# One 512-column product over high and low tokens in the FFN up projections, gated product in PSUM, last up tile one place forward

## What is computed

```
def conv_gated_mlp(hn, w_up, conv_w, conv_b, w_down):
    u = causal_dwconv(hn @ w_up, conv_w, conv_b)
    gate, val = jnp.split(u, 2, axis=-1)
    return (jax.nn.silu(gate) * val) @ w_down
...
        f = (jax.nn.silu(h @ w_ffn_gate[l]) * (h @ w_ffn_up[l])) @ w_ffn_down[l]
```

## Time and profile before

| | us |
|---|---|
| median of 3 runs | 1210.48 (1210.32 to 1210.68) |
| the profiled execution | 1210.57, span 1208.6 |
| PE busy | 1183.3, 98% of the span |
| POOL busy | 881.0, 73% |
| DVE busy | 703.3, 58% |
| ACT busy | 701.7, 58% |

### The profile page before, as it was taken

The page is one execution under the profiler, slowest core; times in us unless marked ns, Lnnn a source line. Parts: engine busy times, 40 slices in busy tenths (PEclk is TensorE's granted clock), DMA queues, the critical chain, the costliest instruction groups (busy, mean ns, idle before and its releaser), DMA issues.

```text
span 1208.6 us, 23310 instructions
## 1 busy us (share of the span) xinstructions
PE 1183.3 (98%) x8146; PEld 1069.2 (88%) x8146; DVE 703.3 (58%) x1520; ACT 701.7 (58%) x1315; POOL 881.0 (73%) x371
## 2 busy tenths in 40 slices
PE   8999999999999999999999999999999999999996
PEld 7998898779999998889999998888798888999995
DVE  5668677456666666546666666293363525444454
ACT  7777677465555557656555656665366445444442
POOL 5847643287988987537889889888786475988882
PEclk9999999999999999999999999999999999999998
DMA  8688522256766656415566665666566344665650
GB/s 284 191 165 201 158 89 89 70 159 207 228 192 190 201 183 187 139 46 164 176 207 190 186 198 158 192 208 193 158 186 196 102 145 119 210 190 177 190 155 36
DMA packets 61354, 202.90 MB, mean 168 GB/s; under 512 B 6480, under 2 KB 13008, under 8 KB 61152
## 3 DMA queue, kind: packets, MB, share of 16 engines
q1 hardware_dynamic: 53712, 193.51, 52.3%
q10 hardware_dynamic: 7568, 8.39, 3.6%
HBM read 197.68 MB, written 4.19 MB: 167 GB/s over the span
## 4 chain that ended last, share of the span: by engine, by line
PE 70%; issue 12%; POOL 10%; DVE 5%; ACT 2%; DMA 0%; POOLq 0%; SPq 0%; DVEq 0%; ACTq 0%
PE bank L183 17%; PE bank L184 16%; PE bank L185 16%; POOL wlo L167 9%; PE solve L185 5%; PE solve L184 5%; PE solve L183 5%; DVE flo L587 1%; ACT whi L163 1%; ACT xhi L306 1%; PE bank L1771 0%; PE bank L1772 0%; DVE resid L2195 0%; PE bank L1468 0%; DVE scr L2190 0%
## 5 line engine op out<-in xcount | busy, mean ns | idle before, releaser
L167 POOL TENSOR_TENSOR wlo<-raw,whi 128x1024 fp32r<-128x1024 f32 x362 | 874.6, 2442 | 294.3 <-ACT whi L163 293.2
L163 ACT ACTIVATE whi<-raw 128x1024 fp32r<-128x1024 f32 x362 | 379.6, 1055 | 134.5 <-PE bank L185 120.0
L183 PE MATMUL bank<-xhi,whi 128*128 128x256 f32 (+1 forms) x936 | 269.8, 288 | 1.2 <-DVE xlo L312 1.0
L184 PE MATMUL bank<-xlo,whi 128*128 128x256 f32 (+1 forms) x936 | 264.6, 283 | 0.0
L185 PE MATMUL bank<-xhi,wlo 128*128 128x256 f32 (+1 forms) x936 | 264.5, 283 | 0.0
L183 PEld LDWEIGHTS bank<-xhi,whi 128*128 128x128 f32 (+1 forms) x936 | 178.3, 190 | 5.2 <-DVE xlo L312 1.3
L183 PE MATMUL bank<-whi,xhi 128*128 128x512 f32 (+2 forms) x456 | 178.2, 391 | 3.1 <-issue 2.0
L184 PEld LDWEIGHTS bank<-xlo,whi 128*128 128x128 f32 (+1 forms) x936 | 178.5, 191 | 1.1
L185 PEld LDWEIGHTS bank<-xhi,wlo 128*128 128x128 f32 (+1 forms) x936 | 178.4, 191 | 0.1
L185 PE MATMUL bank<-whi,xlo 128*128 128x512 f32 (+2 forms) x456 | 173.9, 381 | 0.0
L184 PE MATMUL bank<-wlo,xhi 128*128 128x512 f32 (+2 forms) x456 | 173.7, 381 | 0.0
(11 more groups left out here) (426 smaller groups left out, 1711.4 us busy)
## 6 DMA issues: line engine op xcount, KB each, us to landing
raw<-in_stream SPq DMA_DIRECT2D x363, 512.0 KB, 3.6
band_scratch<-band ACTq DMA_DIRECT2D x1, 3072.0 KB, 35.6
area<-band_scratch ACTq DMA_DIRECT2D x2, 1024.0 KB, 8.9
scr<-in_row_b_gate ACTq DMA_DIRECT2D x1, 1024.0 KB, 6.0
out<-resid SPq DMA_DIRECT2D x4, 256.0 KB, 2.0
tab<-in_tabs SPq DMA_DIRECT2D x1, 640.0 KB, 9.6
resid<-in_x SPq DMA_DIRECT2D x1, 512.0 KB, 3.9
resid<-in_x SPq DMA_DIRECT2D x2, 256.0 KB, 5.0
```

The source lines that it names most:

```text
L163: act.activation(whi[:, n.s, :], raw[:, n.s, :], ACT.Copy).then_inc(hi_ready, 1)
L167: pool.tensor_tensor(wlo[:, n.s, :], raw[:, n.s, :], whi[:, n.s, :].bitcast(F32), ALU.subtract).then_inc(lo_ready, 1)
L183: nc.tensor.matmul(out_ap, a_hi, b_hi, start=start, stop=False)
L184: nc.tensor.matmul(out_ap, a_hi, b_lo, start=False, stop=False)
```

## The change

The high and low tokens become two halves of one tensor `xpair`, 512 columns for each k. In the three FFNs' up projections a k-step is now one matmul of 512 columns (`w_hi` by both halves) and one of 256 (`w_lo` by the high tokens, into the bank's first half), in `both`. The product by the low tokens so lies in columns 256 to 511 of the bank. Behind it ACT copies that half to `ffn_low` in SBUF and calls the unit's `refill` at once, DVE adds it to the first half and scales the sum as before; the rest of a tile is as it was, but the product of gate and val goes to the upper half of the val bank instead of to SBUF. A val bank is written again only once `flo` of the tile two before is done. Up 21 stands before down 17, on PE and in the stream, and the `refill` of down 17 moves into tile 21. Users of `xhi` and `xlo` elsewhere (two helpers of the delta net) only write their slices in another shape; some unused semaphores go.

```diff
@@ -106,8 +106,8 @@
         raw = sb("raw", [P, RING, UNIT])
         whi = sb("whi", [P, RING, UNIT], F32R)
         wlo = sb("wlo", [P, RING, UNIT], F32R)
-        xhi = sb("xhi", [P, 16, SEQ], F32R)
-        xlo = sb("xlo", [P, 16, SEQ], F32R)
+        xpair = sb("xpair", [P, 16, 2 * SEQ], F32R)
+        xhi, xlo = xpair[:, :, 0:SEQ], xpair[:, :, SEQ:2 * SEQ]
         fhi = sb("fhi", [P, 4, SEQ], F32R)
         flo = sb("flo", [P, 4, SEQ], F32R)
         rbc = sb("rbc", [P, SEQ])
@@ -183,6 +183,23 @@
             nc.tensor.matmul(out_ap, a_hi, b_hi, start=start, stop=False)
             nc.tensor.matmul(out_ap, a_hi, b_lo, start=False, stop=False)
             return nc.tensor.matmul(out_ap, a_lo, b_hi, start=False, stop=stop)
+
+        def both(bank, w_hi, w_lo, k, start, stop):
+
+            if stop:
+                nc.tensor.matmul(bank[:, 0:SEQ], w_lo, xhi[:, k, :], start=False, stop=False)
+                return nc.tensor.matmul(bank[:, 0:2 * SEQ], w_hi, xpair[:, k, :], start=False, stop=True)
+            nc.tensor.matmul(bank[:, 0:2 * SEQ], w_hi, xpair[:, k, :], start=start, stop=False)
+            return nc.tensor.matmul(bank[:, 0:SEQ], w_lo, xhi[:, k, :], start=False, stop=False)
+
+        def pairs_still(pe, n, bank, on_the_way=None):
+            pe.wait_ge(lo_ready, n.u + 1)
+            for k in range(KD):
+                w = slice(k * P, k * P + P)
+                mm = both(bank, whi[:, n.s, w], wlo[:, n.s, w], k, k == 0, k == KD - 1)
+                if on_the_way and k == 1:
+                    on_the_way()
+            mm.then_inc(unit_done, 1)
 
         def weights_still(pe, n, outs, kts, xs, on_the_way=None):
 
@@ -434,7 +451,10 @@
                 for n, o in zip(units, outs):
                     pe.wait_ge(lo_ready, n.u + 1)
                     w = slice(k * P, k * P + P)
-                    mm = three(o, whi[:, n.s, w], wlo[:, n.s, w], xhi[:, k, :], xlo[:, k, :], k == 0, k == KD - 1)
+                    if key == "b":
+                        mm = three(o, whi[:, n.s, w], wlo[:, n.s, w], xhi[:, k, :], xlo[:, k, :], k == 0, k == KD - 1)
+                    else:
+                        mm = both(o, whi[:, n.s, w], wlo[:, n.s, w], k, k == 0, k == KD - 1)
                     if k == KD - 1:
                         mm.then_inc(unit_done, 1)
 
@@ -445,11 +465,17 @@
                                start=True, stop=True)
             mm.then_inc(RS.bcast, 1)
 
-        FS = sems("ffn", "scaled first tap conv silu act hi lo")
+        FS = sems("ffn", "low summed scaled first tap conv silu act hi lo")
 
         ffn_g, _o = carve(AREA - 6 * SEQ, 2, SEQ)
         ffn_v, _o = carve(_o, 2, SEQ)
-        ffn_a, _o = carve(_o, 2, SEQ)
+        ffn_low, _o = carve(_o, 2, SEQ)
+
+        def ffn_bank(j, half):
+            return ps[4 + j % 2 * 2 + half]
+
+        def ffn_product(j):
+            return ffn_bank(j, 1)[:, SEQ:2 * SEQ]
         ACC = [[ps[0][:], ps[1][:]], [ps[2][:], ps[3][:]]]
 
         def ffn_unit(f, j, i, what):
@@ -457,22 +483,23 @@
 
             b = BASE[f"ffn{f}"]
             if what == "down":
-                return unit(b + (3 * j + 6 if j < NF - 5 else 3 * j + 8 if j == NF - 5 else 2 * NF + j), 2 * i)
+                return unit(b + (3 * j + 6 if j < NF - 5 else 2 * NF + j), 2 * i)
             half = 0 if what == "gate" else 1
-            return unit(b + half + (2 * j if j < 2 else 3 * j - 2 if j < NF - 2 else 3 * j - 3), 2 * i)
+            return unit(b + half + (2 * j if j < 2 else 3 * j - 2 if j < NF - 2 else 3 * j - 3 if j == NF - 2 else 3 * j - 4), 2 * i)
 
         FKEY = ("ffn0", "ffn1", "ffn2")
 
         def ffn_pe(pe, f, conv, next_key=None):
             s, key, before = FS, FKEY[f], NF * f
-            bank_free, per_tile = (s.conv, 2) if conv else (s.act, 1)
+            gate_free, per_tile = (s.conv, 2) if conv else (s.act, 1)
 
             def up(j, i, on_the_way=None):
                 for half, what in enumerate(("gate", "val")):
-                    if j >= 2:
-                        pe.wait_ge(bank_free, per_tile * (before + j - 2) + 4 * per_tile * i + (half + 1 if conv else 1))
-                    weights_still(pe, ffn_unit(f, j, i, what), [ps[4 + j % 2 * 2 + half][:, 0:SEQ]], KD, 0,
-                                  on_the_way=None if half else on_the_way)
+                    if j >= 2 and half == 0:
+                        pe.wait_ge(gate_free, per_tile * (before + j - 2) + 4 * per_tile * i + 1)
+                    elif j >= 2:
+                        pe.wait_ge(s.lo, before + j - 2 + 4 * i + 1)
+                    pairs_still(pe, ffn_unit(f, j, i, what), ffn_bank(j, half), None if half else on_the_way)
 
             def down(j, i, first=False):
                 pe.wait_ge(s.lo, before + j + 4 * i + 1)
@@ -480,7 +507,7 @@
                 tokens_still(pe, ffn_unit(f, j, i, "down"), ACC, [0], 512, fhi[:, p:p + 1, :], flo[:, p:p + 1, :], first, False)
 
             two_still(pe, key, [ffn_unit(f, 0, 0, what) for what in ("gate", "val")],
-                      [ps[4][:, 0:SEQ], ps[5][:, 0:SEQ]])
+                      [ffn_bank(0, 0), ffn_bank(0, 1)])
             up(1, 0, lambda: bcast_root(pe, key, key, ps[1]))
             up(2, 0)
             pe.wait_ge(RS.copied, RAW[key] + 1)
@@ -491,8 +518,8 @@
                     down(j - 2, i)
             up(19, 0)
             up(20, 0)
+            up(21, 0)
             down(17, 0)
-            up(21, 0)
             down(18, 0)
             down(19, 0)
             pe.wait_ge(s.lo, before + NF)
@@ -504,26 +531,32 @@
 
             def tile_of(j, i):
                 tile, p = j + 4 * i, j % 2
-                for half, (what, dst) in enumerate((("gate", ffn_g), ("val", ffn_v))):
+                for half, (what, dst) in enumerate((("gate", ffn_g[:, p, :]), ("val", ffn_v[:, p, :]))):
                     n = ffn_unit(f, j, i, what)
-                    src = ps[4 + p * 2 + half][:, 0:SEQ]
+                    src = ffn_bank(j, half)[:, 0:SEQ]
+                    act.wait_ge(unit_done, n.u + 1)
+                    if j >= 1:
+                        act.wait_ge(s.summed, 2 * (before + tile - 1) + half + 1)
+                    act.activation(ffn_low[:, half, :], ffn_bank(j, half)[:, SEQ:2 * SEQ], ACT.Copy).then_inc(s.low, 1)
+                    refill(act, n)
                     if conv or half == 0:
                         act.wait_ge(s.scaled, 2 * (before + tile) + half + 1)
                         if j >= 2:
                             act.wait_ge(s.act, before + tile - 1)
                     if conv:
-                        act.activation(dst[:, p, :], src, ACT.Identity, bias=colv(f"bias{f}", tile + half * NF),
+                        act.activation(dst, src, ACT.Identity, bias=colv(f"bias{f}", tile + half * NF),
                                        scale=colv(f"conv{f}", 88 + tile + half * NF)).then_inc(s.first, 1)
                     elif half == 0:
-                        act.activation(dst[:, p, :], src, ACT.Silu).then_inc(s.silu, 1)
-                    refill(act, n)
+                        act.activation(dst, src, ACT.Silu).then_inc(s.silu, 1)
                 if conv:
                     act.wait_ge(s.conv, 2 * (before + tile) + 1)
                     act.activation(ffn_g[:, p, :], ffn_g[:, p, :], ACT.Silu).then_inc(s.silu, 1)
+                if j == NF - 1:
+                    refill(act, ffn_unit(f, NF - 5, 0, "down"))
                 act.wait_ge(s.act, before + tile + 1)
                 if j >= 4:
                     act.wait_ge(unit_done, ffn_unit(f, j - 4, i, "down").u + 1)
-                act.activation(fhi[:, j % 4, :], ffn_a[:, p, :], ACT.Copy).then_inc(s.hi, 1)
+                act.activation(fhi[:, j % 4, :], ffn_product(j), ACT.Copy).then_inc(s.hi, 1)
 
             for j in (0, 1, 2):
                 tile_of(j, 0)
@@ -544,8 +577,6 @@
                     beside(j)
                 if j < 19:
                     refill(act, ffn_unit(f, j - 2, 0, "down"))
-                elif j == 20:
-                    refill(act, ffn_unit(f, 17, 0, "down"))
             refill(act, ffn_unit(f, NF - 4, 0, "down"))
             refill(act, ffn_unit(f, NF - 3, 0, "down"))
 
@@ -553,15 +584,18 @@
             s, key, before = FS, FKEY[f], NF * f
 
             def scaled(j, i, half, what):
-                bank = ps[4 + j % 2 * 2 + half][:, 0:SEQ]
-                dve.wait_ge(unit_done, ffn_unit(f, j, i, what).u + 1)
-                dve.tensor_tensor(bank, bank, rbc[:], ALU.mult).then_inc(s.scaled, 1)
+                bank = ffn_bank(j, half)
+                nth = 2 * (before + j + 4 * i) + half + 1
+                dve.wait_ge(s.low, nth)
+                dve.tensor_tensor(bank[:, 0:SEQ], bank[:, 0:SEQ], ffn_low[:, half, :], ALU.add).then_inc(s.summed, 1)
+                dve.wait_ge(s.summed, nth)
+                dve.tensor_tensor(bank[:, 0:SEQ], bank[:, 0:SEQ], rbc[:], ALU.mult).then_inc(s.scaled, 1)
 
             def tile_of(j, i):
```

(20 more changed lines are left out.)

4 lines of the change are left out of this document (2 added, 2 removed).

## The result

The changed kernel takes **1231.27 us** (median of 4 runs, 1228.92 to 1232.55) against 1210.58 (4 runs, 1210.32 to 1211.96): ratio 1.0168, 95% interval 1.0156 to 1.0180. It is 20.7 us slower; 1231 was forecast.

What follows compares the result with a forecast made beforehand. PE bounds the kernel before; after the change the ACT/DVE loop, held by POOL, binds in FFN 0 and 1. Terms +11.9, +12.3 and -3.65 (FFN 2) sum to +20.6, giving 1231 us; range 1222 to 1240.

Steps and rivals of the forecast that it cites:

- The loop: ACT and DVE's in-order tile work, fhi to fhi: POOL's third unit holds the product, 8.96 us in the conv FFNs.
- When the product is wanted: Conv FFN tile: DVE's product could start 7.5 to 7.95 us after fhi, before 5.65.
- The room before: Kernel before, conv FFN: ACT and DVE take 8.0 us a tile against PE's 8.50, leaving 0.5.
- The sum: Whole kernel: +11.9 in FFN 0, +12.3 in FFN 1, -3.65 in FFN 2, together +20.6 us.
- flo at 0.42: DVE's flo in all 66 tiles: reading the product from PSUM, it always takes 0.42 us.
- PE's saving: Up projections: a k-step falls from 359 to 349 ns, 3.65 us per FFN, worth nothing where ACT and DVE bind.
- The term of FFN 2: FFN 2, without taps: PE stays the bound and its saving shows, -3.65 us.
- The moved up tile: Ends of FFN 0 and 1: up 21 moved forward changes only where PE stands; its moved rounding costs nothing.
- rival C: PE's clock falls in new gaps; low level at the last two downs costs 5.5 us, twice: 1242; 6 in 100.
- Rival A: Conv FFNs: product not held by POOL's third unit, fhi to fhi 8.0 to 8.4, about 1202 us; 14 in 100.

Runs made afterwards that it cites:

- Experiments 2: Also written `no_val_add`: the changed kernel without DVE's add of val's low half in the two conv FFNs; 1228.86 us, ratio 1.0149.
- 3: The changed kernel with DVE's add of val's low half done twice in FFN 0 and 1; 1230.71 us, ratio 1.0162.
- 4: The changed kernel with ACT's copy of the gate's low half ahead of the down unit's rounding, tiles 3 to 19; 1238.23 us, ratio 1.0226.
- 1: The changed kernel with silu of gate in PSUM in the conv FFNs, PE's gate bank waiting for the product; 1205.15 us, ratio to before 0.9956.
- Experiment 6: Also written `up21_back`: the changed kernel with up 21 behind down 17 again and that down's rounding back before tile 21; 1238.23 us, ratio 1.0221.

## Why the forecast was right

**The loop.** Right in place, mechanism and size. 8.96 was forecast; 8.85 is measured in the tile shown. The 0.1 is ACT's 0.28 instead of 0.32 from fhi to the rounding, and POOL's three units in 7.12 instead of 7.20. The mean of the 34 intervals is 8.89, 0.07 under the forecast, and 34 of these are 2.4 of the 3.1 that FFN 0 and 1 were overestimated (10.55 each instead of 11.9 and 12.3). Experiments 2, 3 and 4 show that it is POOL's third unit and not the steps of DVE and ACT; 1 shows that it acts through the product's SBUF inputs. The Trainium skill's page "SBUF — State Buffer", "SBUF: two separate sides", says that a DVE operation with two SBUF inputs takes the lock against a GpSimd operation that reads SBUF. The traces agree: with the output in PSUM in both kernels, 1356 ns with two SBUF inputs and 430 with one. That the output does not matter is the prediction's reading; the section doesn't speak of it, and the product ended 0.28 to 0.33 behind POOL's instruction with its output in SBUF (the kernel before) and 0.29 or 0.30 with it in PSUM.

**When the product is wanted** was put at 7.5 to 7.95 behind fhi; it is 7.45. The gate's copy starts at 1.23 and not 1.39, its add 0.40 behind that and not 0.54, and the scaling 0.47 and 0.45 behind an add and not 0.57. Nothing hangs on it, as 2 and 3 show.

**The room before** was read too large. The 0.5 a tile sets the mean of all 21 intervals (8.0), four of which have no down rounding in front, against PE's tile with a down (8.50). From tile 2 to tile 19 of FFN 0 alone fhi goes from 302.28 to 442.63, 8.26 a tile, so the room was 0.25 there. The sum doesn't use it.

**flo at 0.42** in all 66: right (423 to 427 ns).

**PE's saving.** The mechanism was right, the size was off: 10.4 ns a k-step was taken from the two pitches in long runs of one width, 7.4 is measured: in turn a 512 costs 235 and not 229, and a 256 117 and not 120. The term of FFN 2 was 3.65 and measures 2.6. The formula of the Trainium skill's page "TensorE: Matmul & The Clock Gate", "Back-to-back issue gap", from which the prediction estimated 2.5 ns a k-step and 0.9 per FFN, is further off than the row was, on the other side; the section gives that formula for the isolated gap, and this kernel's matmuls each come with a weight load.

**The moved up tile.** This is the step that failed: up tile and moved rounding were to change only where PE stands. Experiment 6 shows 7 by the medians, of which the loop's part is 4. The sum was not hurt, because tile 21 was counted there as one of four without a down rounding in front (6.87; 6.95 and 6.78 measured), but the sentence that priced the part did not see that this was what the part bought: in the kernel before that rounding did stand in front of tile 21.

**The clock**, rival C, was not to happen in the forecast. It happened in part: in the profiled run not at the last two downs but behind gaps at val of tiles 20 and 21, and the runs are the slower the lower their clock. Its price was too high: 5.5 was put on the low level at the last two downs, and where it came there it cost 1.6 (`no_val_add`) and 1.4 and 2.0 (`up21_back`), since it did not last over the 24 matmuls. The median agrees with 1231 to 0.3 by luck, two errors that cancel: a sum 2.3 too high for the profiled run, and 2.4 between that run and the median, which go with a lower clock that the sum does not have.

**Rival A** was the right one to name. It needed the product free of POOL. Made so, the kernel took 1205 with the stall that the edit brought and 1201 without it, against the forecast's 1202; the loop that nothing holds runs at 7.9, a little under the 8.0 to 8.4 given for it.
